# The experts' rows are added onto the residual in DRAM by indirect adding transfers, one at a time, and the final stage only loads, normalises and stores

## The reference

```python
merged = sigmoid(gate_a) * (y_a @ w_branch_a) + sigmoid(gate_b) * (y_b @ w_branch_b)
h = h + merged @ w_out
h = h + hier_moe(rms_norm(h, norm2_g), ...)   # each token: one group of 4, two experts in it
return rms_norm(h, final_norm_g)

# hier_moe, in short, for token n with experts e1, e2 and weights w1, w2:
y[n] = sum over e in (e1, e2): (silu(x[n] @ w_gate[e]) * (x[n] @ w_up[e]) * w_e) @ w_down[e]
```

## Time and profile before

| | us |
|---|---|
| median of three runs | 3118.31 (3111.61 to 3124.43) |
| profiled execution, own time | 3113.58 |
| its span in the profile | 3111.8 |
| `experts`, from the first turned tile to the end of the block | 2735 to 3028 |
| `finish` | 3028 to 3112 |

### The profile page before, as it was taken

How to read it: one execution, slowest core, us unless ns; L and a number is a source line. 1 busy time by engine, 2 the same in 40 slices (tenths; PEclk the granted TensorE clock), 3 DMA queues, 4 the chain that set the end, 5 groups by cost and what they waited for, 6 DMA issues and landing times. The chain is left out here.

```text
span 3111.8 us, 41114 instructions
## 1 busy us (share of the span) xinstructions
PE 2800.3 (90%) x14110; PEld 1924.4 (62%) x14111; DVE 1682.0 (54%) x3394; ACT 1095.1 (35%) x2270; POOL 1024.5 (33%) x982
## 2 busy tenths in 40 slices
PE   8989999999976799999999899999899999579980
PEld 4668888888864465665545566666444455456760
DVE  6665557655538566666666578887222222422227
ACT  0012222222216355555555456666211122123322
POOL 1266667767713402112130201100222333011116
PEclk9999999999988699999999999999899999789995
DMA  3333235223263101110020111100864243365848
GB/s 131 130 129 109 102 109 178 94 102 109 75 204 152 36 8 59 38 64 13 28 77 20 59 44 41 41 1 1 345 178 111 96 156 136 124 231 208 350 167 312
DMA packets 150215, 355.30 MB, mean 114 GB/s; under 512 B 13840, under 2 KB 61584, under 8 KB 143632
## 3 DMA queue, kind: packets, MB, share of 16 engines
q1 hardware_dynamic: 130016, 280.04, 25.9%
q0 software_dynamic: 13824, 50.34, 4.8%
q10 hardware_dynamic: 6192, 22.55, 1.8%
HBM read 230.52 MB, written 122.36 MB: 113 GB/s over the span
## 5 line engine op out<-in xcount | busy, mean ns | idle before, releaser
L551 ACT ACTIVATE p_kept<-p_a 128x256 f32<-128x256 f32 x336 | 128.5, 383 | 467.3 <-PE p_a L497 440.5
L1510 DVE CUSTOM_DVE_ANT_0 b_prob_s<-b_pq,b_sel 128x640 f32<-128x640 f32 (+5 forms) x192 | 168.6, 911 | 130.2 <-PE b_pq L1402 123.5
L1438 PE MATMUL b_po<-b_probT,vsw 128*64 128x256 f32 (+1 forms) x1824 | 231.7, 372 | 0.0
L1363 POOL TENSOR_TENSOR b_rate<-gates,b_total 128x256 f32<-128x256 f32 x64 | 37.9, 612 | 578.8 <-DVE b_total L1524 578.8
L1805 DVE CUSTOM_DVE_ANT_0 d_prob<-d_pq,d_bias 128x1024 f32<-128x1024 f32 (+6 forms) x192 | 168.0, 909 | 69.6 <-PE d_pq L1697 66.7
L1462 ACT ACTIVATE b_prob_s<-b_prob_s,b_neg 128x1152 f32<-128x1152 f32 (+15 forms) x128 | 152.7, 1194 | 127.4 <-DVE b_neg L1518 127.3
L1402 PE MATMUL b_pq<-ks,b_q 64*128 64x512 f32 (+3 forms) x688 | 164.7, 543 | 16.0 <-DVE b_seg_max L1510 8.6
L1533 DVE COPY b_probT<-b_pt 128x512 f32<-128x512 f32 (+1 forms) x253 | 152.4, 629 | 45.8 <-PE b_pt L1425 45.4
L1697 PE MATMUL d_pq<-d_keys,d_q 64*128 64x512 f32 (+3 forms) x576 | 166.4, 563 | 4.6 <-DVE d_seg_max L1805 3.6
L1425 PE MATMUL b_pt<-ident,b_prob_s 128*128 128x128 f32 x1088 | 158.8, 282 | 7.5 <-DVE b_probT L1533 7.1
L1438 PEld LDWEIGHTS b_po<-b_probT,vsw 128*64 128x64 f32 x1824 | 107.3, 136 | 92.0 <-issue 54.3
(11 more groups left out here) (374 smaller groups left out, 6070.1 us busy)
## 6 DMA issues: line engine op xcount, KB each, us to landing
projT<-p_result SPq DMA_DIRECT2D x64, 512.0 KB, 2.8
y<-e_y ACTq DMA_DIRECT2D x43, 512.0 KB, 4.1
p_w<-in_wt SPq DMA_DIRECT2D x16, 1024.0 KB, 7.2
p_w_more<-in_wt SPq DMA_DIRECT2D x16, 1024.0 KB, 6.4
gates_T<-projT SPq DMA_DIRECT2D x64, 256.0 KB, 4.2
wgu<-in_w_gu SPq DMA_DIRECT2D x4, 4096.0 KB, 15.3
y<-b_q POOLq DMA_DIRECT2D x20, 512.0 KB, 21.5
p_xin<-in_x SPq DMA_DIRECT2D x16, 512.0 KB, 4.0
```

Source lines behind the costliest of these rows:

```text
L1438: mm = nc.tensor.matmul(po[u % 2][g * HD:(g + 1) * HD, o:o + w], s.vsw[:, kb, v0 + g * HD:v0 + (g + 1) * HD], probT[:, f % 4, g * w:(g + 1 ...
L1510: nc.vector.tensor_tensor_reduce(out=to, in0=pq[g][:, 0:nb * P], in1=away, scale=slopes[PAIRS * g + i], scalar=-3e38, op0=ALU.add, op1=ALU ...
```

## The change

The scratch `y`, its zeroing, `s.slot` and the gathers of the final stage are gone. Instead `choose_experts` makes `s.row`: for each tile the list of the rows of `h` to which its 128 results belong. Places with no token point to 128 spare rows that `h` now has behind its 2048. In `experts` POOL adds `e_y[b]` onto those rows of `h` in DRAM by an indirect transfer with an add (`add_rows`). Each one waits for the one before to have landed (`spread`), since two tiles may hold the same token. Two such transfers of zeros stand ahead of the loop, one for each buffer, the second after the first has landed. The load of `h` moves from the end of `experts` into `finish`, tile by tile, six ahead.

```diff
@@ merge_branches
-            nc.gpsimd.memset(zeros, 0.0).then_inc(zeroed, 1)
-            for n in range(2 * NT, MAXT):
-                nc.gpsimd.dma_start(y_t[n], zeros).then_inc(y_cleared, 16)
@@ choose_experts, DVE, behind the index
-            link(nc.vector.tensor_scalar(slot[:], slot[:], float(P), None, ALU.add))
-            link(nc.vector.tensor_copy(s.slot[:], slot[:]))
+            link(nc.vector.tensor_scalar(spare[:], tokens[:, NT - 1:NT], float(P), None, ALU.add))
+            link(nc.vector.tensor_scalar(empty[:], pm[:, 0, :], 0.0, None, ALU.is_equal))
+            link(nc.vector.scalar_tensor_tensor(out=empty[:], in0=empty[:], scalar=spare[:, 0:1], in1=pm[:, 0, :], op0=ALU.mult, op1=ALU.add))
+            nc.vector.tensor_scalar(s.row[:, 0:1], spare[:], -1.0, None, ALU.add)
+            nc.vector.tensor_scalar(s.row[:, 1:MAXT + 1], empty[:], -1.0, None, ALU.add)
@@ experts, SP
-            for k in range(4):
-                sp.dma_start(s.h[:, 4 * k:4 * k + 4, :], h_t[:, 4 * k:4 * k + 4, :]).then_inc(h_in, 16)
-            sp.wait_ge(h_in, 16 * 4)
@@ experts, POOL
+            def add_rows(i, b):
+                nc.gpsimd.tensor_copy(to[b][:], s.row[:, bass.ds(2 * i + b, 1)]).then_inc(row_ready, 1)
+                pool.wait_ge(row_ready, 2 * i + b + 1)
+                pool.wait_ge(y_copied, 4 * i + 2 * b + 4)
+                pool.wait_ge(spread, 32 * i + 16 * b + 32)
+                nc.gpsimd.indirect_dma_start(d["h"], bass.IndirectOffsetOnAxis(ap=to[b][:], axis=0), y[b][:], None,
+                                             compute_op=ALU.add).then_inc(spread, 16)
+            for b in range(2):
+                nc.gpsimd.memset(y[b][:], 0.0).then_inc(blank, 1)
+                nc.gpsimd.tensor_copy(to[b][:], s.row[:, 0:1]).then_inc(blank, 1)
+                pool.wait_ge(blank, 2 * b + 2)
+                if b == 1:
+                    pool.wait_ge(spread, 16)
+                nc.gpsimd.indirect_dma_start(d["h"], ..., y[b][:], None, compute_op=ALU.add).then_inc(spread, 16)
             with pool.Fori(1, ends[NG] + 1) as i:
                 for b in range(2):
                     pool.wait_ge(x_turned, 2 * i + b - 1)
                     fetch(nc, pool, d, s, b, s.index[:, bass.ds(2 * i + b, 1)], 2 * i + b + 1)
+                    add_rows(i - 1, b)
+            add_rows(ends[NG], 0)
+            pool.wait_ge(spread, 32 * ends[NG] + 48)
@@ experts, ACT (and DVE alike, without the store)
-                act.wait_ge(y_stored[b], 16 * i + 16)
+                act.wait_ge(spread, 32 * i + 16 * b + 16)
                 nc.scalar.activation(y[b][:, 0:512], py[0][:], ACT.Copy).then_inc(y_copied, 1)
-                act.wait_ge(y_copied, 4 * i + 2 * b + 4)
-                act.dma_start(y_t[2 * i + b], y[b][:]).then_inc(y_stored[b], 16)
@@ finish
+            load(0)
+            load(1)
             sp.dma_start(gain[:], d["final_row"]).then_inc(gain_in, 16)
+            for t in range(2, AHEAD):
+                load(t)
             for t in range(NT):
                 sp.wait_ge(done, t + 1)
+                if t + AHEAD < NT:
+                    load(t + AHEAD)
                 sp.dma_start(out_t[t], h[:, t, :]).then_inc(stored, 16)
-                    nc.gpsimd.indirect_dma_start(y[:, t % NB, k, :], None, d["y"], ...s.slot[:, t, k:k + 1]...)
-                nc.vector.tensor_tensor(pair[:, 0, :], pair[:, 0, :], pair[:, 1, :], ALU.add).then_inc(paired, 1)
-                nc.vector.tensor_tensor(h[:, t, :], h[:, t, :], pair[:, 0, :], ALU.add).then_inc(added, 1)
```

More of the change, by code:

```diff
@@ L28 @@
 MAXT = 52
-NSLOT = MAXT * P
 RMS_EPS, SUBLN_EPS = 1e-6, 1e-5
@@ L2595, in _ @@
             ends = register_ends(pool)
+            def add_rows(i, b):
+                nc.gpsimd.tensor_copy(to[b][:], s.row[:, bass.ds(2 * i + b, 1)]).then_inc(row_ready, 1)
+                pool.wait_ge(row_ready, 2 * i + b + 1)
+                pool.sem_inc(step, 1)
+                pool.wait_ge(y_copied, 4 * i + 2 * b + 4)
+                pool.sem_inc(step, 1)
+                pool.wait_ge(spread, 32 * i + 16 * b + 32)
+                pool.sem_inc(step, 1)
+                nc.gpsimd.indirect_dma_start(d["h"], bass.IndirectOffsetOnAxis(ap=to[b][:], axis=0), y[b][:], None,
[6 more added lines that the diff above has]
+                    pool.wait_ge(spread, 16)
+                nc.gpsimd.indirect_dma_start(d["h"], bass.IndirectOffsetOnAxis(ap=to[b][:], axis=0), y[b][:], None,
+                                             compute_op=ALU.add).then_inc(spread, 16)
             with pool.Fori(1, ends[NG] + 1) as i:
@@ L2667, in _ @@
             store(ends[NG], 0)
-            act.wait_ge(y_stored[0], 16 * ends[NG] + 32)
-            act.sem_inc(step, 1)
-            act.wait_ge(y_stored[1], 16 * ends[NG] + 16)
-            act.sem_inc(step, 1)
         @block.vector
@@ L2676, in _ @@
             dve.sem_inc(y_copied, 2)
-            for b in range(2):
-                dve.sem_inc(y_stored[b], 16)
             nc.vector.memset(hidT[:], 0.0).then_inc(hidT_ready, 1)
@@ L2688, in copy_y @@
                 dve.wait_ge(y_ready, 2 * i + b + 1)
-                dve.wait_ge(y_stored[b], 16 * i + 16)
+                dve.sem_inc(step, 1)
+                dve.wait_ge(spread, 32 * i + 16 * b + 16)
                 nc.vector.tensor_copy(y[b][:, 512:D], py[1][:]).then_inc(y_copied, 1)
@@ L2721, in finish @@
         gain_in = nc.alloc_semaphore("f_gain_in")
-        y_in = [nc.alloc_semaphore(f"f_y_in{b}") for b in range(NB)]
+        h_in = [nc.alloc_semaphore(f"f_h_in{b}") for b in range(AHEAD)]
         stored = nc.alloc_semaphore("f_stored")
-        paired, added, ss_ready, var_ready, rstd_ready, done = (nc.alloc_semaphore("f_" + n) for n in (
-            "paired", "added", "ss_ready", "var_ready", "rstd_ready", "done"))
+        ss_ready, var_ready, rstd_ready, done = (nc.alloc_semaphore("f_" + n) for n in ("ss_ready", "var_ready", "rstd_ready", "done"))
+        h_t = d["h"][0:T].rearrange("(n p) c -> n p c", p=P)
         out_t = out[0].rearrange("(n p) c -> n p c", p=P)
@@ L2738, in _ @@
         def _(pool):
-            def fetch(t):
-                if t >= NB:
-                    pool.wait_ge(added, t - NB + 1)
-                for k in range(2):
-                    nc.gpsimd.indirect_dma_start(y[:, t % NB, k, :], None, d["y"], bass.IndirectOffsetOnAxis(ap=s.slot[:, t, k:k + 1], axis=0)).then_inc(y_in[t % NB], 16)
-            for t in range(NB - 1):
-                fetch(t)
             for t in range(NT):
-                if t + NB - 1 < NT:
-                    fetch(t + NB - 1)
                 pool.wait_ge(var_ready, t + 1)
@@ L2755, in _ @@
             for t in range(NT):
-                act.wait_ge(added, t + 1)
+                act.wait_ge(h_in[t % AHEAD], 16 * (t // AHEAD + 1))
                 if t >= 1:
@@ L2775, in _ @@
             dve.wait_ge(gain_in, 16)
-            add(0)
             for t in range(NT):
-                if t + 1 < NT:
-                    add(t + 1)
                 dve.wait_ge(ss_ready, t + 1)
@@ L2903, in program @@
         s.index = sb(ctx, "index", [P, MAXT], mybir.dt.int32)
+        s.row = sb(ctx, "row", [P, MAXT + 1], mybir.dt.int32)
         s.weight = sb(ctx, "weight", [P, MAXT])
```

42 lines of the change are left out of this document (16 added, 26 removed).

## The result

The change makes the kernel slower by 0.8%: 3141.5 us (median of five runs, 3135.9 to 3145.7) against 3116.7 of the kernel before on the same chip, ratio 1.0081, 95% interval 1.0067 to 1.0096. The profiled execution took 3135.9 us with a span of 3134.1, 22.3 us more than the span of before. The forecast was 3108.

The account below looks back on a forecast made before the run. PE was taken to bound the experts, transfers and their chain the final stage. Terms 0.7 + 0 + 9.5 + 7 - 1.8 + 4.5 - 30 = -10.1 us gave 3108 against 3118.3; range 3086 to 3165.

Parts of the forecast that it names:

- the likeliest case: Whole kernel: the forecast of 3108 us against 3118.3, chance 0.45, by itself a range of 3092 to 3122.
- Undisturbed steps: Experts away from weight loads: steps stay at 6.16 us, an add landing in 5.3 us; priced at 0.
- 1.1 us are left: Undisturbed steps: the gather behind the add leaves 3.9 us later, its rows still landing 1.1 us before they are needed.
- Rival 1: Undisturbed steps: adds slower than a step, at 7.4 us landing net +47, 3165 us; decides from L (landing) = 6.6; chance 0.25.
- Start of the experts: First gathers: transfers of zeros beside the weights delay tile 2; +9.5 us, bounds +4 and +18.
- Two later loads: Later weight loads of the experts: gathers leave 3.9 us later behind an add; +3.5 us each, +7, bounds 0 and 16.
- -1.8 for h: Third weight load: the load of h no longer runs beside it, saving 1.8 us.
- End of the experts: Last two adds: the last waits for the one before, then lands 5.3 us later, at 3032.8; +4.5 us.
- Final stage: After the experts: 33 tiles moved instead of 49, 53 us instead of 83.6; -30 us, -23 at today's rate, -35 without gaps.
- Routing +0.7: Routing before the experts: DVE loses two small operations and gets five; +0.7 us.
- zeroing 0: Beside the merge: removing twenty stores and one memset is worth 0, since PE had no idle time there.

Follow-up runs that it names:

- e13: e3 with TensorE's read of the next step's expert number (`pick`) moved behind the gate and up matmuls of the step before; 3132.1 us, steps 6.40 us.
- e17: e13 with every gather also issued ahead of the add it stood behind; steps 6.15 us; timed again at 3108.5 us, ratio 0.9975 to the kernel before.
- e22: e17 without the early `pick` read: two targets and chains, gathers ahead of the adds; steps 6.56 us, no whole time given.
- e1: The changed kernel with its two 128-row transfers of zeros replaced by one plain 2 KB write to a spare row; 3125.4 us.
- e2: e1 with every gather issued one half-step ahead of the add it stood behind; 3125.2 us, steps 6.81 us.
- e5: e1 without blanks, adds and every wait for them, so the output lacks the experts' share; 3072.7 us.
- e4: e1 with indirect transfers that write the rows instead of adding them, so the output lacks the residual; 3102.9 us.
- e3: e1 with odd steps' rows added into a second tensor, each target with its own chain, both summed in the final stage; 3142.0 us, ratio 1.0087.
- e20: Against e1, no adds: each expert row written to its own row of a tensor, loaded directly and added in the final stage; 3147.8 us, ratio 1.0099.
- e14: e1 with adds cut into column halves, a chain each, gathers ahead of the adds and `pick` read a step early; 3126.0 us, ratio 1.0039.
- e9: e1 with ACT instead of GpSimd waiting for the last add at the end of the experts; 3133.2 us.
- e15: e14 with ACT waiting for the last adds and issuing the final stage's first six loads itself; 3130.2 us, ratio 1.0048.

## Why the prediction was wrong

The range, 3086 to 3165, holds the result; the likeliest case and the way do not. The final stage gave 8.4 us more than forecast, which hid part of what the other steps had wrong. By its own steps:

- **Undisturbed steps, priced at 0: the step that failed.** Measured +0.83 a step, 25.6 us over 31 steps. "It costs nothing if issue to landing is under 6.16 us less some 0.3 us for the semaphore and the waits" had both terms off. From the landing to the next issue it is 0.75 us, not 0.3 (an allowance that no row of the kernel before gave), and the landing took 6.2 us, not 5.3 (inside the 5.1 to 6.3 that I gave). 6.97 us of chain don't fit into 6.16. The 0.75 could have been read before: it is the 0.79 us of idle time between list copy and gather, which I took for the price of a list and not for that of every wait ahead of a software transfer.
- **"1.1 us are left" for the gather** behind the add was wrong as well, by little: with two chains and the read ahead, issuing it first was worth 0.25 us a step (e13 to e17). That the gather itself was late there, and not something else behind it in that order, PE's waits don't show.
- **A cause I did not have at all:** the read of `pick` by TensorE's sequencer, 0.30 us before and 1.2 to 1.3 as a rule in the change. Alone it costs 0.4 us a step (e22). The timeline did not show it, since register instructions are not counted there.
- **Rival 1** (the add is slower than a step) named the place, POOL waiting at `spread`, and had the right sign. Its deciding point of L = 6.6 us was too high, since it used the same 0.3 us; the result came with a landing of 6.2.
- **Start of the experts, +9.5.** The second long wait ended 9.0 us later than before (28.7 us after the first turn, 19.6 before). Right in size, half right in cause: the blanks cost 4.1 us (e1), the gather behind the first add 6.9 (e1 to e2, which ends 2.7 under before). The times in between were off both ways: the first zeros left at 2733.90, not at 2737.9, and the gather at 2743.54, ahead of the 2745 to 2756 forecast, but its rows were waited for until 2762.34, 18.8 us where I had taken 16 for the worst.
- **Two later loads, +7, and -1.8 for h.** Measured +4.7 and +10.0, with -2.2 for h in the second (e5). Load 3 was mis-sized by 8 us: the gather behind the add was taken to cost "2 to 3 us more", and the chain, which does the same by itself (e2), nothing. Most of both is the single transfer and its waits, not the adding (e4: +3.5 and +6.5).
- **End of the experts, +4.5.** Measured +13.4. The landing chain was counted with 5.3 us an add; it is 6.97 and then 6.2. And GpSimd's drain, 4.1 us, comes out of its cover when GpSimd is the last engine; I did not price it. Plain writes would have left 9.5 of the 13.4 (e4).
- **Final stage, -30.** Measured -38.4, beyond the bound of -35: the stage took 45.2 us, 2 more than its bytes at 403 GB/s, where I had added 5 us for both ends and a tenth for gaps.
- **Routing +0.7 and zeroing 0** can't be told from the spread of the first turn, -1.3 us.

## What to carry to other kernels

A chain of dependent transfers must be priced from issue to issue, with the wait's reaction in it (here 0.75 us), and compared with the step it must fit into; then ask what else the same transfer slows, its issuing engine's next instructions and the register reads of other engines among them. When several such limits lie within 10% of each other, removing one shows almost nothing, and two edits worth 3 and 4 us of the experts' time each can be worth 28 together (e2, e3 and e22 against e1): test the combination before dropping either. Work moved to the issuing engine also moves the end of its stage: what it drains last, everybody waits for.

## What the runs showed of the hardware

- In these traces an indirect transfer that adds 128 rows of 4 KB holds the DMA engines 2.7 times as long as one that writes them (0.499 x 7 against 0.213 x 6 us) and lands in 6.1 against 3.3 us; GpSimd's issue takes 1.60 against 0.99 us. Half the bytes land in 4.9 to 5.2.
- A register read from SBUF by TensorE's sequencer takes 0.30 us, and 0.31 beside indirect writes (e4, median of the last nine). Beside an add it depends on when it begins: 2.1 to 3.3 us after the start of the add's issue it took 0.83 to 1.52 us (33 of 34 reads of the change), sooner or from 4.4 us on 0.30 to 0.32 (46 reads), though the add lands only after 6. The path on which the two meet was not found. The Trainium skill (DMA: Bandwidth & Descriptors, "Latency and other measured facts") gives a floor of about 600 ns for a `tensor_load`, the name under which the trace has this read; the trace has half of that, and twice it under adds.
- GpSimd's drain at the end of a stage ended 10.0 to 10.7 us after its last whole indirect transfer was issued, whether that was an add (10.35 in the change, 9.97 in e1) or a write that had landed long before (10.54 in e4, whose drain took 7.09 us, and 10.73 in e20, 7.17 us). So 4.1 us after the landing is what is left for an add, and a faster landing alone would not end the stage sooner. It was 8.6 us after the last gather before the change and 7.9 after the last half in e14. Where ACT waited for the landing it ended 9.5 us after the issue in e9 and 5.4 in e15. Why it takes so long, and why it was shorter in e15, is open.
